# Input projections reordered and block attention's values moved into the rotation steps

## What is computed

```python
h = x @ w_cols                                   # 1024 -> 3400 (layer 1: 3432) columns
gq, gk, gv, gg, galr        = split(h_gla)       # gated linear attention, 4 heads
rr, rk, rv, rwlr, ralr, rglr = split(token_shift_mix(h_rwkv, mu))   # delta-rule recurrence
q, kc, vc, ks, vs, kw, vw, gate = split(h_nsa)   # block attention: compressed, selected, window
o_gla, o_rwkv, o_nsa = three mixers
x = layer_norm(alpha * x + concat(o_gla, o_rwkv, o_nsa) @ w_out)
x = layer_norm(alpha * x + gated feed-forward(x))
```

## Time and profile before

| quantity | value |
|---|---|
| median of 3 runs | 2021.17 us (2020.33 to 2023.05) |
| profiled execution, its own time | 2023.03 us |
| its span, first to last instruction | 2021.2 us |
| TensorE busy | 1966.1 us, 97% of the span |
| VectorE busy | 855.1 us, 42% |
| ScalarE busy | 313.4 us, 16% |
| GpSimd busy | 45.1 us, 2% |
| mean granted TensorE clock | 0.993 of full speed |
| L402 / L419 in the chain that ended last | 6% / 2% of the span |
| L361 (unread products) in that chain | 2% of the span |

### The profile page before, as it was taken

How to read it: one execution, slowest core, us unless ns; L and a number is a source line. 1 busy time by engine, 2 the same in 40 slices (tenths; PEclk the granted TensorE clock), 3 DMA queues, 4 the chain that set the end, 5 groups by cost and what they waited for, 6 DMA issues and landing times.

```text
span 2021.2 us, 24513 instructions
## 1 busy us (share of the span) xinstructions
PE 1966.1 (97%) x9835; PEld 1115.1 (55%) x9835; DVE 855.1 (42%) x1538; ACT 313.4 (16%) x725; POOL 45.1 (2%) x62
## 2 busy tenths in 40 slices
PE   8999999999999999999999999999999999999997
PEld 7878588748777588749553333333333333333332
DVE  1487588865587586754731111111111111111112
ACT  1335211101435111103410000000000000000001
POOL 0021000000021000000000000000000000000000
PEclk9999999999999999999999999999999999999999
DMA  8540067646630165436298999999999999999996
GB/s 332 217 158 1 32 234 308 251 167 278 263 126 1 41 226 199 171 154 266 89 393 373 428 429 429 427 429 429 427 430 427 430 429 427 429 427 430 429 428 287
DMA packets 44275, 598.75 MB, mean 296 GB/s; under 512 B 5056, under 2 KB 5360, under 8 KB 8464
## 3 DMA queue, kind: packets, MB, share of 16 engines
q1 hardware_dynamic: 44208, 597.82, 71.9%
HBM read 596.73 MB, written 1.07 MB: 296 GB/s over the span
## 4 chain that ended last, share of the span: by engine, by line
PE 82%; DMA 15%; DVE 3%; issue 0%; ACT 0%; SPq 0%; DVEq 0%
PE ps L2349 18%; DMA ring<-in_stream 15%; PE ps L1404 12%; PE ps L2397 8%; PE ps L1489 7%; PE ps L402 6%; PE ps L2323 3%; PE ps L1273 3%; PE ps L361 2%; PE ps L2338 2%; PE ps L419 2%; PE ps L2434 2%; PE ps L1820 1%; PE ps L1986 1%; PE ps L1150 1%; PE ps L1167 1%
## 5 line engine op out<-in xcount | busy, mean ns | idle before, releaser
L2349 PE MATMUL ps<-ring,HT 128*64 128x512 f32 x2176 | 479.4, 594 | 20.0 <-DMA ring<-in_stream 19.2
L2349 PEld LDWEIGHTS ps<-ring,HT 128*64 128x64 f32 x2176 | 152.9, 137 | 340.1 <-issue 289.3
L2397 PE MATMUL ps<-SB,HT 128*64 128x512 f32 x1088 | 249.2, 612 | 0.9 <-ACT HT L2460 0.9
L2505 DVE TENSOR_SCALAR HT<-ps 128x512 f32<-128x512 f32 x34 | 23.5, 692 | 449.8 <-PE ps L2349 449.8
L2397 PEld LDWEIGHTS ps<-SB,HT 128*64 128x64 f32 x1088 | 77.0, 140 | 170.2 <-issue 170.2
L1404 PE MATMUL ps<-ring,SB 128*128 128x256 f32 x704 | 156.0, 379 | 0.3 <-DVE SB L331 0.3
L2454 ACT ACTIVATE HT<-HT 128x512 f32<-128x512 f32 x34 | 21.5, 631 | 843.9 <-DVE HT L2505 843.9
L1404 PEld LDWEIGHTS ps<-ring,SB 128*128 128x128 f32 x704 | 133.6, 190 | 18.8 <-issue 0.7
L2517 DVE TENSOR_TENSOR HT<-ps,TOK 128x512 f32<-128x512 f32 x34 | 23.5, 692 | 281.3 <-PE ps L2397 281.3
L402 PE MATMUL ps<-SB,ring 128*128 128x256 f32 x576 | 126.9, 384 | 1.3 <-DMA ring<-in_stream 1.3
L402 PEld LDWEIGHTS ps<-SB,ring 128*128 128x128 f32 x576 | 110.8, 193 | 17.1 <-issue 1.6
(11 more groups left out here) (489 smaller groups left out, 2251.8 us busy)
## 6 DMA issues: line engine op xcount, KB each, us to landing
ring<-in_stream SPq DMA_DIRECT2D x210, 2048.0 KB, 16.6
SB<-in_stream SPq DMA_DIRECT2D x68, 2048.0 KB, 24.8
SB<-in_ln SPq DMA_DIRECT2D x8, 512.0 KB, 7.0
CST<-in_const SPq DMA_DIRECT2D x1, 1362.0 KB, 5.5
PAR<-in_layer SPq DMA_DIRECT2D x2, 558.5 KB, 11.6
X<-in_x SPq DMA_DIRECT2D x1, 1024.0 KB, 4.9
HN<-in_head_norm SPq DMA_DIRECT2D x2, 512.0 KB, 12.8
SB<-in_cond_row SPq DMA_DIRECT2D x2, 512.0 KB, 10.9
```

What stands on the lines that cost most here:

```text
L2349: m = pe.matmul(ps[HD * half:HD * (half + 1), a, :], XE[:, 2 * b + k, q * SLOTS_E:(q + 1) * SLOTS_E], w[:, k, a, half, :], start=False, st ...
L2397: m = pe.matmul(ps[HD * c:HD * (c + 1), 3, :], EHT[:, k, HD * b:HD * (b + 1)], w[:, k, c, :], start=b + k == 0, stop=b + k == 4, skip_grou ...
```

## The change

The feature tiles are renumbered: r, k, v, w/a, misc come first (groups 0 to 4), then gq and gk (5, 6), keys and queries (7 to 10). `mix_dve` waits for five copies instead of seven. TensorE's order becomes: groups 0 to 8, `gla_gate_pe`, `rwkv_ranks_pe`, groups 9 and 10, `rwkv_norm_pe`, group 11 (now the 24 gate columns alone, 16 products), group 12 (tokens, before 13), rope, group 13. ScalarE copies group 9 after `rwkv_gates_act` and before `gla_query_act`. vs and vw become group 14: 16 products of 256 columns in rotation steps 2 and 3, where unread products stood, with a copy by ScalarE in step 3 that TensorE awaits before the turn. Slot in 5 is released only then, so in order behind it come the slots wo 0, wo 1, gu 0 and gu 1. The compressed blocks (`N_FL`) move to another part of SBUF, and `cmp_pool` on GpSimd waits for `rw_ops` instead of the last projection.

```diff
-T_GQ, T_GK, T_R, T_K, T_V, T_WA, T_G1, T_MISC, T_VC, T_KC, T_KS, T_KW, T_Q = 0, 2, 4, 6, 8, 10, 11, 12, 13, 14, 15, 16, 17
+T_R, T_K, T_V, T_WA, T_G1, T_MISC, T_VC, T_GQ, T_GK, T_KC, T_KS, T_KW, T_Q = 0, 2, 4, 6, 7, 8, 9, 10, 12, 14, 15, 16, 17
...
-                return "proj_ready", 15 * l + [2, 4, 6, 8, 10, 13, 15][s]
+                return "proj_ready", 15 * l + [2, 4, 6, 8, 10, 15, 14][s]
...
-            return g % 4 if g < 13 else g - 9
+            return g % 4 if g < 12 else (4, 5, 3)[g - 12]
...
+        def project_gates_pe(pe, l):
+            w = slot(AT["in", l, 5]).rearrange("p (k n) -> p k n", k=KT)
+            pe.wait_ge(S("proj_evac"), 15 * l + 8)
+            for t in range(NT):
+                for k in range(KT):
+                    m = pe.matmul(ps[:, proj_bank(11), 24 * t:24 * (t + 1)], XT[:, k, t * P:(t + 1) * P], w[:, k, 384:408],
+                                  start=k == 0, stop=k == KT - 1)
+            m.then_inc(S("proj_ready"), 1)
...
+        def project_values_pe(pe, l, t, ks):
+            w = slot(AT["in", l, 5]).rearrange("p (k n) -> p k n", k=KT)
+            for k in ks:
+                m = pe.matmul(ps[:, proj_bank(14), t * 256:(t + 1) * 256], XT[:, k, t * P:(t + 1) * P], w[:, k, P:P + 256],
+                              start=k == 0, stop=k == KT - 1)
+            if t == NT - 1 and ks[-1] == KT - 1:
+                m.then_inc(S("proj_ready"), 1)
...
         def mix_dve(v, l, I, L):
-            v.wait_ge(S("proj_evac"), 15 * l + 7)
+            v.wait_ge(S("proj_evac"), 15 * l + 5)
...
-        N_FL = [view(flat_xt, 1024 + 512 * i, [16, 32]) for i in range(2)]
+        N_FL = [view(SB, 10240 + 512 * i, [16, 32]) for i in range(2)]
...
             pool.wait_ge(S("rope"), ROPE_PIECES * l + 1)
-            pool.wait_ge(S("proj_ready"), 15 * (l + 1))
+            pool.wait_ge(S("rw_ops"), l + 1)
...
@@ mixers_pe @@
                 if s == GLA_BACK:
-                    clock_pe(pe, 3, 0, 256, 3)
+                    project_values_pe(pe, l, 0, range(4))
...
+                if s == GLA_BACK + 1:
+                    project_values_pe(pe, l, 1, range(4, 8))
                 if h < HALF_LEVELS:
                     inverse_update_pe(pe, l, h)
...
                 if s == GLA_BACK:
-                    clock_pe(pe, 3, 0, 256, 3)
+                    project_values_pe(pe, l, 0, range(4, 8))
+                    project_values_pe(pe, l, 1, range(2))
                     back_pe(pe, 2 * l, G_XC, 4)
-                    clock_pe(pe, 3, 0, 256, 3)
+                    project_values_pe(pe, l, 1, range(2, 4))
...
                     if u == 1:
-                        clock_pe(pe, 3, 0, 256, 6)
+                        pe.wait_ge(S("proj_evac"), 15 * (l + 1))
+                        clock_pe(pe, 3, 0, 256, 2)
                         pe.wait_ge(S("cmp_kv"), l + 1)
...
@@ mixers_act @@
+                if u == 1:
+                    project_act(act, l, (14,))
...
@@ block.tensor @@
-                    project_pe(pe, l, range(5))
+                    project_pe(pe, l, range(9))
...
                 gla_gate_pe(pe, l)
                 rwkv_ranks_pe(pe, l)
-                project_pe(pe, l, (5,))
+                project_pe(pe, l, (9,))
+                project_pe(pe, l, (10,))
                 rwkv_norm_pe(pe, l)
-                project_pe(pe, l, (6,))
+                project_gates_pe(pe, l)
+                project_tokens_pe(pe, l, 0, range(KT))
+                for p in range(2):
+                    rope_pe(pe, l, p)
+                project_tokens_pe(pe, l, 1, range(KT))
...
@@ block.scalar @@
                 rwkv_ranks_act(act, l, I)
-                project_act(act, l, (9,))
                 gla_decay_act(act, l, L)
                 rwkv_gates_act(act, l, I)
-                project_act(act, l, (10,))
+                project_act(act, l, (9,))
                 gla_query_act(act, l)
-                project_act(act, l, (11, 12))
+                project_act(act, l, (10, 11))
                 rwkv_decay_act(act, l, I)
                 rwkv_values_act(act, l)
-                project_act(act, l, (13,))
+                project_act(act, l, (12,))
                 gla_key_act(act, l, 0)
                 gla_key_act(act, l, 1)
-                project_act(act, l, (14,))
+                project_act(act, l, (13,))
```

More of the change, by code:

```diff
@@ L383, in project_first_pe, with project_pe @@
                     m.then_inc(S("proj_ready"), 1)
-        def project_pe(pe, l, slots):
-            def bank_free(g):
-                if g >= 13:
+        def project_pe(pe, l, groups):
+            for g in groups:
+                need_slot(pe, AT["in", l, g // 2])
+                w = slot(AT["in", l, g // 2]).rearrange("p (k n) -> p k n", k=KT)
+                if g >= 4:
+                    pe.wait_ge(S("proj_evac"), 15 * l + g - 3)
+                for j in range(2 if g < 10 else 1):
+                    for k in range(KT):
+                        m = pe.matmul(ps[:, proj_bank(g), j * T:(j + 1) * T],
+                                      w[:, k, (2 * (g % 2) + j) * P:(2 * (g % 2) + j + 1) * P],
+                                      XT[:, k, :], start=k == 0, stop=k == KT - 1)
+                m.then_inc(S("proj_ready"), 1)
@@ L389, in bank_free @@
                     pe.wait_ge(S("gla_zb"), l + 1)
                     pe.wait_ge(S("rw_gates"), l + 1)
[L391 to L421, removed]
@@ L430, in project_act @@
                     to, n = HT[:, 20, :], T
-                elif g < 13:
-                    to, n = NV[:, g - 11, :], 280
-                else:
-                    to, n = TOK[:, g - 13, :], 512
-                nc.scalar.activation(to, ps[:, proj_bank(g), 0:n], ACT.Copy,
-                                     scale=HD ** -0.5 if g == 0 else 1.0).then_inc(S("proj_evac"), 1)
+                elif g == 11:
+                    to, n = NV[:, :, 256:280], 48
+                elif g < 14:
+                    to, n = TOK[:, g - 12, :], 512
+                else:
+                    to, n = NV[:, :, 0:256], 512
+                come = ps[:, proj_bank(g), 0:n]
+                if g in (11, 14):
+                    come = come.rearrange("p (t c) -> p t c", t=NT)
+                nc.scalar.activation(to, come, ACT.Copy,
+                                     scale=HD ** -0.5 if g == 5 else 1.0).then_inc(S("proj_evac"), 1)
         def mix_dve(v, l, I, L):
-            v.wait_ge(S("proj_evac"), 15 * l + 7)
+            v.wait_ge(S("proj_evac"), 15 * l + 5)
             v.wait_ge(S("par_loaded"), 32 * (l + 1))
@@ L499, in gla_scores_pe @@
             if tc == 0:
-                pe.wait_ge(S("proj_evac"), 15 * l + 13)
+                pe.wait_ge(S("proj_evac"), 15 * l + 12)
             for h in range(4):
@@ L741, in rwkv_current_pe @@
         def rwkv_current_pe(pe, l):
-            pe.wait_ge(S("proj_evac"), 15 * l + 14)
+            pe.wait_ge(S("proj_evac"), 15 * l + 13)
             for t in range(NT):
@@ L753, in rwkv_pairs_pe @@
             if u == 0:
-                pe.wait_ge(S("proj_evac"), 15 * (l + 1))
+                pe.wait_ge(S("proj_evac"), 15 * l + 14)
             if u >= 2:
@@ L999, in rope_pe @@
                 pe.wait_ge(S("rw_init"), l + 1)
+                pe.wait_ge(S("proj_evac"), 15 * l + 11)
             first, n = rope_tiles(p)
```

21 lines of the change are left out of this document (16 added, 5 removed).

## The result

The changed kernel takes 2032.42 us (median of 4 runs, 2031.27 to 2034.12), the kernel before 2022.11 us on the same chip (4 runs, 2020.33 to 2023.53): ratio 1.0063, 95% interval 1.0051 to 1.0075. It is slower, by more than the predicted range allowed. The profiled executions are 2031.6 and 2023.03 us long, their spans 2029.8 and 2021.2 us.

What follows compares the result with a forecast made beforehand. TensorE was taken to bound the projections and to be level with VectorE in early rotation steps. Projections of -2.0 and +0.4 us plus 2 x 1.3 in the rotation took 2021.17 to 2022.2 us; range 2017.5 to 2026.5.

Steps and rivals of the forecast that it cites:

- Removed and added in the projections: TensorE's projections: groups 11 and 12 save 7.55 us, the gate group costs 3.5, so -4.05 us a layer.
- The cover that goes: Projections: new TensorE waits, 2.0 us (layer 0) and 3.4 (layer 1) for ranks, 0.9 to 1.0 for layer 1's values.
- Moved into the rotation: Rotation steps 2 and 3: value products delay `back_pe` and the turn by 1.3 us a layer.
- The sum: Whole kernel: projections -2.0 and +0.4 us plus twice 1.3 in the rotation, +1.0 us, giving 2022.2 us.
- rival 4: TensorE's clock falls in the projections' new waits: 2025.5 us with one fall, 2028.8 with two; chance 0.12.
- Rivals 2, 3 and 5: Rotation costs nothing, 2019.6 us (0.13); new waits don't appear, 2015.7 (0.10); waits add up further in mixers, 2024.8 (0.15).
- The rest: POOL's blocks start some 4 us earlier, the later weight loads stay hidden, the expert block's transfers shift along; no cost added.
- stays level: Projections: VectorE's chain to `rw_ops` and the first rope pieces keeps up with TensorE's new times; costed at nothing.

Runs made afterwards that it cites:

- e4_back: Changed kernel with `back_pe` ahead of the six value products of rotation step 2: 2031.05 us, ratio 1.0055.
- e3_fill_inter: Changed kernel with unread products ahead of the rank wait and the gate products dealt between those of group 10: 2021.02 us, ratio 1.0007.
- b1_gap: Kernel before with only group 9 moved behind the rank products, its ScalarE copy behind the gates: 2034.16 us, ratio 1.0072.
- b2_narrow: Kernel before with groups 11 and 12 computed as products of 256 columns, then 16 of 24 columns in a row: 2023.93 us, ratio 1.0025.
- e12_end: Changed kernel, group 9 before ranks, gates dealt into group 10, `back_pe` early, unread products in two waits and more in four late rotation steps: 2031.12 us.
- e7b_again: Changed kernel with group 9 before ranks, gates dealt into group 10, `back_pe` ahead of the value products, profiled again: 2022.65 us, ratio 1.0015.

## Why the prediction was wrong

**Removed and added in the projections.** Right. The 16 gate products take 3.5 us, and 7.55 us of groups 11 and 12 are gone.

**The cover that goes.** Right in place and length: 1.96, 3.39 and 1.10 us for 2.0, 3.4 and 1.0, and no wait at the value transposes in layer 0. The table load is 1.28 us with the function straight behind it in the new trace as well.

**Moved into the rotation.** Right in amount (1.29 us a layer) and in path: `back_pe` comes 1.31 us later, VectorE's unbroken 7.5 us behind it pass that on, and ScalarE's copy of group 14 holds nothing up. What the prediction didn't say is how near a second path lies. With `back_pe` early, in e4_back, 0.44 us come back and no more, because 36 records instead of 30 stand on TensorE.

**The sum.** This is the step that failed. It priced each new wait at its own length and left TensorE's pace behind it as it was, and the clock stood in rival 4 with 0.12. The clock fell in both layers, twice in each. Layer 0's way from group 8 to the mixers is 5.0 us longer than the sum said (+3.0 for -2.0), layer 1's 9.2 us (+9.6 for +0.4). e3_fill_inter, without the falls, comes back to the sum within 0.4 us in each layer (its layer 1 without the 1.0 us wait), and b1_gap, with the rank waits and nothing else, loses as much as the whole change.

**Rival 4.** Right in kind, too small in chance and in size. I took 3.3 us for a fall from one window of the expert block and stopped at two. A spell there was 6.8 us long; here there were four, 30.7 us together. Half of that would be 15.4 us; the two layers lost 14.2. The evidence that made me doubt it, small products at a clock of 1.00 in 1018 to 1026 us, has no wait in it and shows only one stretch. I also priced the gate group at its 3.5 us only; as 16 narrow products (32 records) in a row it has a further price, a spell of 6.8 us of half clock in layer 1 and of 3.4 in layer 0. The Trainium skill, "TensorE: Matmul & The Clock Gate", section "HAM oscillation — how this bites in real kernels", says that idle gaps throttle TensorE again; the traces agree for the waits of 3.4 us in each of the four executions profiled, and for those of 2.0 us in three of four. Spells without a wait (b2_narrow, e12_end) are not covered by it.

**Rivals 2, 3 and 5.** None happened: the rotation cost 1.3 us, the waits were there, and the way from turn to mixing projections is 55.5 us as before.

**The rest.** One thing that I costed at nothing isn't free, and it hides behind the falls. I wrote that VectorE's chain "stays level" with TensorE. With the cover restored that chain is the floor: it gives 2.1 us of the 4 in layer 0 and 0.6 in layer 1. So even a version without a fall could not have won the 4.05 us a layer.

## What to carry to other kernels

A wait on TensorE costs more than its length: ask what kind of products follow it, because with a wait of 2.0 to 3.4 us ahead of the small rank products the clock halved here for 7 to 14 us of a stretch in which TensorE is the limit. A group of wide products between a producer and its reader is cover, and narrow products should be dealt between wide ones rather than put in a row. Before counting work taken from one engine as gain, follow the next engine's unbroken chain to the same point; the shorter of the two slacks is what there is to win.

## What the runs showed that was not expected

- The clock fell for 20.5 us behind a wait of 0.39 us at the end of the rotation (three profiles), and once with no wait in the stretch at all (e12_end at 534.5 us). Products on few rows or with few columns stood ahead of each; whether they are the cause is not shown.
- The same instructions at the same place have half clock in one execution and full clock in the next. The versions with the cover restored have executions 13 to 26 us apart (e7b_again 2015.3 to 2039.4 us), so their median says little without the granted clock beside it.
- In the clock's record of the expert block, where transfers and products run evenly, both kernels have short spells of 3.4 us (before at 1623.0, 1681.1 and 1739.1 us) that neither the change nor any experiment here explains.
